# Feed-forward norm's root moved behind the gate and up products of a two-block transformer kernel

## What is computed

```python
def rms_norm(x, g):
    xf = x.astype(jnp.float32)
    y = xf * lax.rsqrt(jnp.mean(xf * xf, axis=-1, keepdims=True) + RMS_EPS)
    return (y * g.astype(jnp.float32)).astype(x.dtype)

def swiglu_ffn(x, w_in, w_out):
    gu = jnp.einsum("bsd,df->bsf", x, w_in)
    h = jax.nn.silu(gu[..., :D_FF]) * gu[..., D_FF:]
    return jnp.einsum("bsf,fd->bsd", h, w_out)

h = h + swiglu_ffn(rms_norm(h, ffn_norm[layer]), ffn_w_in[layer], ffn_w_out[layer])
```

## Time and profile before

| | |
|---|---|
| median of 3 runs | 1321.41 us (1318.88 to 1325.15) |
| the profiled execution | 1322.12 us, span 1320.3 us |
| TensorE busy | 1147.0 us (87%) |
| VectorE busy | 635.5 us (48%) |
| ScalarE busy | 412.8 us (31%) |
| DMA | 362.47 MB, mean 275 GB/s |
| stages (span time) | layer 0 mixer to 99, its feed-forward to 297, attention to 433, its feed-forward to 630, second block's attentions to some 850, experts to the end |

### The profile page before, as it was taken

One profiled execution on the slowest core, in us unless ns is written; L12 is line 12 of the kernel. 1 busy time (PEld: TensorE's weight loads), 2 busy tenths in 40 slices (PEclk: granted clock), 3 DMA queues, 4 the chain that ended last, 5 costly groups with the idle time before them and its releaser, 6 DMA issues.

```text
span 1320.3 us, 22956 instructions
## 1 busy us (share of the span) xinstructions
PE 1147.0 (87%) x9320; PEld 926.9 (70%) x9321; DVE 635.5 (48%) x997; ACT 412.8 (31%) x519; POOL 32.7 (2%) x71
## 2 busy tenths in 40 slices
PE   9999999999989999999899999777766768567666
PEld 8999999998968999999798998643322323223222
DVE  5797777775344454556455787452221112111213
ACT  3765333334474443335433665330000000000001
POOL 0000000000000000000100000000000000000000
PEclk9999999999999999999899999989888889888889
DMA  9676988874530865550754334689999999999996
GB/s 350 218 284 209 333 299 298 301 267 138 185 124 1 303 208 171 180 189 32 136 192 145 114 137 154 256 354 422 428 429 428 429 429 428 429 428 429 429 428 265
DMA packets 99401, 362.47 MB, mean 275 GB/s; under 512 B 4161, under 2 KB 51665, under 8 KB 84113
## 3 DMA queue, kind: packets, MB, share of 16 engines
q1 hardware_dynamic: 95216, 335.06, 66.7%
q0 software_dynamic: 3984, 26.50, 5.0%
q10 hardware_dynamic: 144, 0.10, 0.0%
HBM read 360.58 MB, written 1.06 MB: 274 GB/s over the span
## 4 chain that ended last, share of the span: by engine, by line
PE 68%; DMA 21%; DVE 5%; ACT 2%; issue 2%; SPq 0%; DVEq 0%; POOL 0%; POOLq 0%; ACTq 0%
DMA wbuf<-in_w_up 21%; PE ps L1764 19%; PE ps L1687 10%; PE ps L1662 8%; PE ps L2064 7%; PE ps L1940 4%; PE ps L1652 3%; PE ps L1696 3%; PE ps L1671 3%; PE ps L1631 2%; PE ps L2114 2%; PE ps L2084 1%; DVE parts L1069 1%; PE ps L1836 1%; PE ps L1721 1%
## 5 line engine op out<-in xcount | busy, mean ns | idle before, releaser
L1069 DVE TENSOR_TENSOR parts<-wbuf,parts 128x2048 fp32r<-128x2048 f32 x88 | 200.3, 2290 | 135.6 <-ACT parts L811 50.8
L1764 PE MATMUL ps<-big_parts,parts 128*128 128x256 f32 x2112 | 259.6, 285 | 5.1 <-DVE big_parts L1069 5.1
L1764 PEld LDWEIGHTS ps<-big_parts,parts 128*128 128x128 f32 x2112 | 257.6, 192 | 5.8 <-issue 5.8
L2064 PE MATMUL ps<-wbuf,big 128*32 128x256 f32 x2176 | 166.8, 473 | 106.7 <-DMA wbuf<-in_w_up 98.4
L2064 PEld LDWEIGHTS ps<-wbuf,big 128*32 128x32 f32 x2176 | 86.4, 134 | 201.3 <-issue 95.2
L1687 PE MATMUL ps<-big_parts,parts 128*128 128x256 f32 x1152 | 142.7, 283 | 1.7 <-DVE parts_f L1274 1.1
L1687 PEld LDWEIGHTS ps<-big_parts,parts 128*128 128x128 f32 x1152 | 140.0, 190 | 2.1 <-issue 1.3
L1001 ACT ACTIVATE big<-ps 128x128 f32<-128x128 f32 x33 | 9.2, 278 | 419.1 <-PE ps L2064 419.1
L1578 DVE TENSOR_TENSOR big<-big,ps 128x128 f32<-128x128 f32 x33 | 9.5, 288 | 262.8 <-ACT big L1001 262.8
L1662 PE MATMUL ps<-parts_f,parts 128*128 128x256 f32 x672 | 97.2, 284 | 0.0
L1662 PEld LDWEIGHTS ps<-parts_f,parts 128*128 128x128 f32 x672 | 87.8, 192 | 0.3 <-issue 0.2
(11 more groups left out here) (319 smaller groups left out, 1409.7 us busy)
## 6 DMA issues: line engine op xcount, KB each, us to landing
wbuf<-in_w_down SPq DMA_DIRECT2D x32, 2048.0 KB, 38.0
wbuf<-in_w_gate SPq DMA_DIRECT2D x31, 2048.0 KB, 32.6
wbuf<-in_w_up SPq DMA_DIRECT2D x31, 2048.0 KB, 37.1
wbuf<-in_ffn_w_in SPq DMA_DIRECT2D x44, 1024.0 KB, 10.9
wbuf<-in_w_ada POOLq DMA_DIRECT2D x24, 1024.0 KB, 8.5
wbuf<-in_ffn_w_out SPq DMA_DIRECT2D x22, 1024.0 KB, 5.0
wbuf<-in_w_in SPq DMA_DIRECT2D x10, 2048.0 KB, 8.2
wbuf<-in_attn_w_qkv SPq DMA_DIRECT2D x6, 2048.0 KB, 8.4
```

Of the source, the lines that this page charges most:

```text
L1069: nc.vector.tensor_tensor(lo, whole, hi.bitcast(F32), ALU.subtract).then_inc(done, 1)
L1764: ins = mm(ps[:, b, d * 256:(d + 1) * 256], w[pw][:, k, d * P:(d + 1) * P], h_part_of[px][:, k], start=(k == 0 and d == 0 and i == 0), sto ...
L2064: ins = mm(at, rows, gu_place[s][:, :, k, r * P:(r + 1) * P], start=(k == 0), stop=(k == KC - 1))
```

## The change

The products no longer run on the normed residual but on residual times the norm's weights; the root, which depends only on the token, is applied to the gate and the up halves when they leave PSUM. The order changes with it:

- ScalarE makes the upper part of each chunk straight from `xT`, as Identity with the weight column as scale, behind each bank's addition; VectorE makes the lower part in one operation, x times weight minus upper part (`scaled_low`).
- VectorE adds the four quarters of squares into one (`add_squares`, three additions of 128x512), and TensorE sums only two chunks (`sums_of_two`), between the gate and the up half of step 0, into bank 3 instead of 0.
- In each step VectorE multiplies the gate half by the root into `hid` (Silu then runs in place, in SBUF), and the up half into a new place, `up_scaled`; the product of the two is formed from SBUF.
- In layer 0 VectorE's split of step 0's up weights moves ahead of the additions, adaLN unit 0 behind the sum of squares.

```diff
-SUM_BANK = (7, 0, 0, 0, 0, 0, 0, 4)
+SUM_BANK = (7, 3, 0, 3, 0, 0, 0, 4)
...
             def ffn_norm(n, layer):
-                norm_square(n)
+                for b in range(4):
+                    act.wait_ge(x_ready, 4 * (n - 1) + b + 1)
+                    for k in range(2 * b, 2 * b + 2):
+                        nc.scalar.activation(h_part_of[0][:, k], xT[:, k], ACT.Identity, scale=col(R_FFN + KC * layer + k)).then_inc(fh_hi, 1)
+                    nc.scalar.activation(squares[n][:, 2 * b:2 * b + 2], xT[:, 2 * b:2 * b + 2], ACT.Square).then_inc(sq_done, 1)
                 norm_root(n)
-                for k in range(KC):
-                    act.wait_ge(h_part, KC * layer + k + 1)
-                    nc.scalar.activation(h_part_of[0][:, k], hT[:, k], ACT.Copy).then_inc(fh_hi, 1)
...
+                    act.wait_ge(ffn_gate_scaled, n + 1)
+                    nc.scalar.activation(hid[:, s], hid[:, s], ACT.Silu).then_inc(ffn_silu, 1)
                     act.wait_ge(ffn_gu, n + 1)
-                    nc.scalar.activation(hid[:, s], ps[:, 2 * s, :], ACT.Silu).then_inc(ffn_silu, 1)
...
+            def scaled_low(layer, b):
+                for k in range(2 * b, 2 * b + 2):
+                    dve.wait_ge(fh_hi, fh_before[layer] + k + 1)
+                    nc.vector.scalar_tensor_tensor(out=h_part_of[1][:, k], in0=xT[:, k], scalar=col(R_FFN + KC * layer + k), in1=h_part_of[0][:, k].bitcast(F32),
+                                                   op0=ALU.mult, op1=ALU.subtract).then_inc(fh_lo, 1)
+            def add_squares(n):
+                into = squares[n][:, 0:2]
+                for b in range(1, 4):
+                    dve.wait_ge(sq_done, 4 * n + b + 1)
+                    ins = nc.vector.tensor_tensor(into, into, squares[n][:, 2 * b:2 * b + 2], ALU.add)
+                    if b < 3:
+                        link(ins)
+                ins.then_inc(sq_added, 1)
...
             dve.wait_ge(silu_c, 1)
+            split_u(0, 0)
+            for b in range(4):
+                add_biased(b)
+                dve.wait_ge(x_ready, b + 1)
+                scaled_low(0, b)
+            add_squares(1)
             ada_unit(0)
...
                 def step(s, n, following=True):
+                    dve.wait_ge(ffn_g, n + 1)
+                    nc.vector.tensor_tensor(by_token(hid[:, s]), by_token(ps[:, 2 * s, :]), root, ALU.mult).then_inc(ffn_gate_scaled, 1)
                     if following:
                         split_g(1 - s, n + 1)
...
+                    dve.wait_ge(ffn_gu, n + 1)
+                    nc.vector.tensor_tensor(by_token(up_scaled), by_token(ps[:, 2 * s + 1, :]), root, ALU.mult).then_inc(ffn_hid, 1)
+                    dve.wait_ge(ffn_hid, 2 * n + 1)
                     dve.wait_ge(ffn_silu, n + 1)
-                    nc.vector.tensor_tensor(hid[:, s], hid[:, s], ps[:, 2 * s + 1, :], ALU.mult).then_inc(ffn_hid, 1)
+                    nc.vector.tensor_tensor(hid[:, s], hid[:, s], up_scaled, ALU.mult).then_inc(ffn_hid, 1)
...
-            ffn_norm(1, 0, lambda k: col(R_FFN + k))
+            dve.wait_ge(root_done, 2)
             ffn(0)
...
-            add_residual("wo1")
-            ffn_norm(3, 1, lambda k: col(R_FFN + KC + k))
+            for b in range(4):
+                add_bank("wo1", b)
+                dve.wait_ge(x_ready, 4 * 2 + b + 1)
+                scaled_low(1, b)
+            add_squares(3)
+            dve.wait_ge(root_done, 4)
             ffn(1)
...
-                gate_up(0, base, wait_rows=True)
-                gate_up(1, base + 1)
+                gate_up(0, base, sums_of_two, wait_rows=True)
+                gate_up(1, base + 1, root_read)
...
-            norm_sums(1)
             ffn(0)
```

More of the change, by code:

```diff
@@ L1187, in _ @@
             nc.vector.tensor_copy(hidden_half, not_before).then_inc(mask_ready_half, 1)
[L1189 to L1194, removed]
-                nc.vector.nop().then_inc(h_ready, KC)
-            dve.wait_ge(silu_c, 1)
-            ada_unit(0)
@@ new lines, in add_squares, with add_biased @@
+            def add_squares(n):
[6 more added lines that the diff above has]
+                ins.then_inc(sq_added, 1)
+                nc.vector.nop().then_inc(h_ready, KC)
+            def add_biased(b):
+                wait_bank(dve, "lo1", b)
+                for k in range(2 * b, 2 * b + 2):
+                    ins = nc.vector.scalar_tensor_tensor(out=xT[:, k], in0=ps[:, 4 + k // 2, (k % 2) * 256:(k % 2 + 1) * 256], scalar=col(R_BOUT + k),
+                                                         in1=xT[:, k], op0=ALU.add, op1=ALU.add)
+                ins.then_inc(x_ready, 1)
@@ L1208, in add_residual, with add_bank @@
+            def add_bank(last, b):
+                wait_bank(dve, last, b)
+                ins = nc.vector.tensor_tensor(xT[:, 2 * b:2 * b + 2], ps[:, 4 + b, :].rearrange("p (k t) -> p k t", k=2), xT[:, 2 * b:2 * b + 2], ALU.add)
+                ins.then_inc(x_ready, 1)
             def add_residual(last):
                 for b in range(4):
-                    wait_bank(dve, last, b)
-                    ins = nc.vector.tensor_tensor(xT[:, 2 * b:2 * b + 2], ps[:, 4 + b, :].rearrange("p (k t) -> p k t", k=2), xT[:, 2 * b:2 * b + 2], ALU.add)
@@ L1766, in half, with gate_up, sums_of_two, root_read @@
                     return ins
-                def gate_up(slot, step, wait_rows=False):
+                def gate_up(slot, step, between=None, wait_rows=False):
                     pe.wait_ge(fg_lo, step + 1)
                     half(fg_part, 2 * slot, wait_rows).then_inc(ffn_g, 1)
+                    if between is not None:
+                        between()
                     pe.wait_ge(fu_lo, step + 1)
                     half(fu_part, 2 * slot + 1, False).then_inc(ffn_gu, 1)
+                n = 2 * layer + 1
+                def sums_of_two():
+                    pe.wait_ge(sq_added, layer + 1)
+                    for k in range(2):
+                        ins = mm(ps[:, SUM_BANK[n], 0:SEQ], ones, squares[n][:, k], start=(k == 0), stop=(k == 1))
+                    ins.then_inc(sum_done, 1)
+                def root_read():
+                    pe.wait_ge(root_done, n + 1)
                 def down(slot, step, first=False, last=False):
@@ L1867, in _ @@
             accumulate_by_bank(part_terms(unit_parts("wo1"), 4, lambda px, k: o_part[px][:, 4 + k]))
-            norm_sums(3)
             ffn(1)
```

20 lines of the change are left out of this document (15 added, 5 removed).

## The result

The changed kernel takes 1312.6 us (median of 6 runs, 1310.4 to 1315.1) against 1322.1 for the kernel before beside it (1318.5 to 1325.2): ratio 0.994, 95% interval 0.9915 to 0.9966. By the ratio that is 8 us less, by its interval 4.5 to 11, by the two medians 9.5; the forecast of 1315.4 was 2.8 us too high, inside its range. The profiled execution took 1315.1 us (span 1313.4), the slowest of its six.

The account below looks back on a forecast made before the run. TensorE was taken to set the pace up to the mixture of experts, expert weights after. Gains of 4.2 (layer 0) and 3.3 (layer 1) less 1.5 (clock) made 6.0 us: 1321.4 to 1315.4, range 1310.5 to 1318.8.

Parts of the forecast that it names:

- Step 1 and 2: Feed-forward entry: 23.91 us of TensorE without waits; in layer 0, 6.65 us less minus 2.4 of waits, gaining 4.2.
- step 5: Clock: both entry gaps go, with 1.6 us each already counted; the new 3.2 us wait in layer 1 costs 1.5.
- Step 3: Layer 1's entry: parts and squares in time, step 1's gate weights 0.3 us late; entry gain 6.5 us.
- Step 4: Layer 1, product step 2: its weights come late, a 3.2 us wait before the third gate half; layer 1 gains 3.3.
- clock stays up: Rival: no clock drop at layer 1's 3.2 us wait for step 2's weights; gain 7.5 us, 1313.9, chance 0.18.
- Step 6: Feed-forward product steps: the new multiplies on VectorE are covered, steps stay 17.28 us; cost zero.
- Step 7: Last product steps of both layers: the added multiplies cost zero, with 0.2 to 0.3 us left to spare.
- Step 8: Load queues: adaLN unit 0 runs 13 us later, delaying POOL's load of unit 2; cost zero.
- What TensorE gains earlier should pass to the end undiminished.: TensorE's progress releases the experts' loads, so time gained before the experts was to reach the end in full.
- VectorE as the bound: Rival: in layer 0 VectorE's multiplies set the step, from 2.0 us each; at 2.9, 19.1 us steps, 1335, chance 0.05.
- The test that I set myself: Sign of error: time between 640 us and the end changes by over 2 us.

Follow-up runs that it names:

- the padded kernel: Changed kernel plus 12 unused fp32 products of constants (24 passes) in TensorE's idle time behind the router's logits: 1309.1 us, ratio 0.9914.
- the first pair of the table: First profiled executions, kernel before against changed kernel: spans 1320.3 and 1313.4 us; the second pair, both run again unedited: 1317.6 and 1309.6 us.
- both moves and the padding: Changed kernel with km and vm loaded behind step 2's weights (layer 1), layer 0's additions a quarter ahead, and 12 unused TensorE products: 1302.2 us, ratio 0.9841.

## Why the prediction was right, point by point

- *Step 1 and 2, layer 0.* Waits of 0.50, 0.62 and 0.77 us, forecast 0.53, 0.84 and 1.06, 0.5 too much in all. The upper part took 501 ns, as taken, 84 more than the Copy's 417, and no second charge for the zero bias shows. The Trainium skill's page "ScalarE: Activation LUTs" (What ACT_TABLE_LOAD costs) has 93 ns for one pointer operand, 9 more than measured here. The entry as a whole still came to the forecast 26.3, since the pieces between the waits took 0.5 more (the four passes 1.13 us with their start, not 0.87). First down product at 125.4, forecast 125.3. The size of the gain was half luck: 4.2 us against the profile of before, which has the clock drop, 2.9 against the one that has not. The old entries' gap lowered the clock in five of the six that three profiles show, so step 5's reading of it was fair, and its size a mean at best.
- *Step 3.* Wait 0.57 instead of 0.3.
- *Step 4.* The forecast's best part. Step 2's products began 33.1 us after the end of the bank products (458.23 - 425.14), forecast 33.0; the wait was 2.91 against 3.2, the gain 3.2 against 3.3. Moving the loads proved the cause.
- *Step 5, the clock at step 2.* Charge 1.5, measured 13.17 - 11.66 = 1.5. But it doesn't come each time: in five profiles with a wait of 2.9 to 3.1 us there, the clock fell in three and stayed in two (the padded kernel, 3.14 us, and the one with five more multiplies, 2.97). By these five the rival "clock stays up" was worth some 0.4 and not 0.18. By the Trainium skill's page "TensorE: Matmul & The Clock Gate" (Part 1), which has the rate fall only after an idle window, none of these partly idle waits would cost; three of five did.
- *Step 6.* The multiplies cost nothing, as said, and the cover is real. But "zero" was not the sum: steps came out 0.19 us shorter, 1.6 to 2 us a layer, and the new places in SBUF allow it, which I had read in the diff and costed at nothing. This is the term that failed, with its sign on the kernel's side. I had named longer steps as a sign of error and never thought of shorter ones.
- *Step 7.* The forecast left 0.2 to 0.3 us to spare; nothing is left. The parts were done at 284.75 us in layer 0, and TensorE's next product began at 284.89, 0.26 us behind the one before it instead of 0.12; in layer 1 0.24 instead of 0.12. The last steps trail by 0.1 us each.
- *Step 8.* Nothing waited for adaLN loads.
- *"What TensorE gains earlier should pass to the end undiminished."* Wrong by 3 to 4 us. The stall in the last expert comes with the shorter program. Two misses of opposite sign, 3.2 to 4 us for the shorter products of both layers and these 3 to 4 us, partly cancel, and so the sum of 6.0 came nearer to the spans (6.9 us less in the first pair of the table, 8.0 in the second) than its terms deserved. Nor are the spans made of the forecast's terms alone: 1.6 us of the first pair lie between recurrence and attention and 4.2 of the second in the attentions of the second block, both rows of clock drops. Without these two rows the pairs give 5.4 and 3.9 us. The mechanism of both entries is shown; that the total came out so close was in part luck.

The rivals: none of them took over. VectorE as the bound was measured, at 17.93 us a step. The test that I set myself (time behind 640 us changing by over 2 us) is met: experts +3.6, attentions between 0 and -4.

## What to carry to other kernels

Look at what a restructured entry leaves in the DMA queue: the chain showed that the gain would be eaten by a load, and swapping two lines of the queue returned 4.8 us, more than either entry had gained. Where two engines hand quarters to each other, issue the next quarter's first operation ahead of this quarter's last one. And compare the end of the profile even for a change in the middle: a program that is a few dozen instructions shorter can stall elsewhere. The best version here, both moves and the padding, is at 0.984 of the kernel before.

## What the hardware did that I had not expected

- 128x256 fp32r products came at two steady paces, 120.0 and 118.7 ns, both with the clock at 1.00. The faster one appeared only where the moving operand's parts lie 128 bytes beyond a multiple of 512 from the work area's start (12 layers of 16, against 0 of 6).
- With a fetch of instructions TensorE stopped for 2.1 to 3.2 us in the last expert, and up to 6.6 us were lost where the clock fell behind it. One or two stalls of 3.5 to 5.2 us of TensorE stand in the first experts of every profile, in five of them one of VectorE of 5.2 to 7.2 us as well. Padding with 24 idle passes took the last one away.
- The same gap lowered the clock in some executions and not in others: 2.53 us at the old entries in five of six, 2.9 to 3.1 us at step 2 in three of five; a gap of 1.35 us in the same place didn't, in the one profile that has it.
